# Forgetting attention in three units per head pair, output product joined to the next scores

## The reference, cut to what matters

```python
c = jnp.cumsum(log_f, axis=1)                 # forget gates, summed over the tokens
logits = einsum('bqhd,bkhd->bhqk', q_b * dh ** -0.5, k) + c_b[..., None] - c_k
logits = jnp.where(key_pos <= q_pos, logits, -inf)
o_fox = einsum('bhqk,bkhd->bqhd', softmax(logits), v)
...
o_fox = rms_norm(o_fox, fox_norm)             # over the 64 values of each head
h = h + concatenate([o_gla, o_fox]) @ w_out
```

## Time and profile before

| | |
|---|---|
| time, median of 3 | 2253.59 us (2252.46 to 2253.8) |
| the profiled execution | 2252.86 us |
| its span | 2251.6 us |
| TensorE busy | 2230.4 us, 99% of the span |
| VectorE, ScalarE busy | 63%, 47% |
| TensorE clock granted | 1.00 |

### The profile page before, as it was taken

How to read it: one execution, slowest core, us unless ns; L and a number is a source line. 1 busy time by engine, 2 the same in 40 slices (tenths; PEclk the granted TensorE clock), 3 DMA queues, 4 the chain that set the end, 5 groups by cost and what they waited for, 6 DMA issues and landing times.

```text
span 2251.6 us, 39369 instructions
## 1 busy us (share of the span) xinstructions
PE 2230.4 (99%) x15807; PEld 2025.2 (90%) x15807; DVE 1410.6 (63%) x2601; ACT 1048.9 (47%) x1963; POOL 118.3 (5%) x203
## 2 busy tenths in 40 slices
PE   9999999999999999999999999999999999999998
PEld 7798999999997898999899888978899888998997
DVE  5356576759743465667689566869455455863664
ACT  5356554447633465544377443223244444552652
POOL 3001010000000001100000010110000000000001
PEclk9999999999999999999999999999999999999999
DMA  6555676246434435732355262777721222543651
GB/s 222 163 130 148 179 190 184 98 141 174 137 94 127 121 112 142 185 118 96 112 174 167 87 181 82 192 188 216 197 66 64 67 95 86 154 156 117 182 165 51
DMA packets 97112, 313.01 MB, mean 139 GB/s; under 512 B 13809, under 2 KB 17811, under 8 KB 95907
## 3 DMA queue, kind: packets, MB, share of 16 engines
q1 hardware_dynamic: 84627, 220.93, 30.4%
q0 software_dynamic: 11584, 88.25, 16.9%
q10 hardware_dynamic: 720, 1.31, 0.2%
HBM read 308.32 MB, written 86.02 MB: 175 GB/s over the span
## 4 chain that ended last, share of the span: by engine, by line
PE 93%; DVE 3%; ACT 2%; issue 1%; DMA 0%; POOL 0%; SPq 0%; ACTq 0%; DVEq 0%; POOLq 0%
PE G L1427 58%; PE G L1464 15%; PE G L1543 7%; PE X L1464 3%; PE X L1755 1%; PE X L1710 1%; PE X L1840 1%; PE X L1733 1%; DVE wL L2432 1%; PE X L1824 1%; ACT wH L1893 1%; PE X L1503 1%; PE X L1809 1%; PE X L1427 1%; PE X L1796 0%
## 5 line engine op out<-in xcount | busy, mean ns | idle before, releaser
L1893 ACT ACTIVATE wH<-raw 128x512 fp32r<-128x512 f32 (+3 forms) x693 | 475.0, 704 | 468.8 <-PE G L1427 388.5
L2432 DVE TENSOR_TENSOR wL<-raw,wH 128x512 fp32r<-128x512 f32 (+3 forms) x693 | 538.3, 788 | 238.5 <-ACT wH L1893 235.1
L1427 PE MATMUL G<-aH,wH 128*128 128x264 f32 (+2 forms) x2000 | 503.0, 316 | 2.5 <-DVE aL L2445 2.0
L1427 PE MATMUL G<-aL,wH 128*128 128x264 f32 (+2 forms) x2000 | 481.7, 306 | 0.0
L1427 PE MATMUL G<-aH,wL 128*128 128x264 f32 (+2 forms) x2000 | 481.6, 306 | 0.0
L1427 PEld LDWEIGHTS G<-aH,wH 128*128 128x128 f32 x2000 | 324.5, 189 | 28.1 <-issue 6.0
L1427 PEld LDWEIGHTS G<-aH,wL 128*128 128x128 f32 x2000 | 322.4, 188 | 17.2
L1427 PEld LDWEIGHTS G<-aL,wH 128*128 128x128 f32 x2000 | 322.9, 188 | 14.4 <-issue 0.2
L1464 PE MATMUL G<-seven,wH 128*128 128x256 f32 (+2 forms) x960 | 177.5, 284 | 1.6 <-DVE wL L2432 1.5
L2591 DVE TENSOR_TENSOR hT<-G,hT 128x528 f32<-128x528 f32 (+1 forms) x83 | 58.0, 699 | 183.0 <-PE G L1427 183.0
L1464 PEld LDWEIGHTS G<-seven,wH 128*128 128x128 f32 x960 | 148.1, 188 | 3.7 <-issue 2.9
(11 more groups left out here) (407 smaller groups left out, 3911.0 us busy)
## 6 DMA issues: line engine op xcount, KB each, us to landing
raw<-weights SPq DMA_DIRECT2D x195, 512.0 KB, 3.8
weight_sums<-weights POOLq DMA_DIRECT2D x72, 704.0 KB, 6.4
raw<-weight_sums SPq DMA_DIRECT2D x160, 256.0 KB, 2.9
raw<-weights SPq DMA_DIRECT2D x48, 704.0 KB, 4.1
raw<-weights SPq DMA_DIRECT2D x121, 256.0 KB, 2.9
weight_sums<-weight_sums POOLq DMA_DIRECT2D x24, 704.0 KB, 5.2
weight_sums<-weights POOLq DMA_DIRECT2D x24, 448.0 KB, 4.9
raw<-weights SPq DMA_DIRECT2D x12, 384.0 KB, 5.4
```

The source lines that it names most:

```text
L1427: done = e.matmul(m.pair(i)[0:M, bank, 0:n], a[:, k, 0:M], b[:, kx, lo - t0:lo - t0 + n], start=(k == 0 and c == 0), stop=(k == nk - 1 and ...
L1893: e.activation(m.high(i)[:, c], m.raw(i)[:, c], ACT.Copy).then_inc(s.w_hi, 1)
L2432: e.tensor_tensor(m.low(i)[:, c], m.raw(i)[:, c], m.high(i)[:, c].bitcast(F32), ALU.subtract).then_inc(s.w_lo, 1)
```

## The change

- `FOX` groups the tiles into three units a pair, u = 0 to 11: kind 0 is tiles 1 and 2 in one (tile 2's scores at column 160 of the same bank), kind 1 is tile 3, kind 2 tile 4. Kind 0's scores, exponentials and normalisations have three pieces a head (144, 272 and the 16 meta queries).
- The transposes of both heads are taken in rounds of four: 3, 2 and 3 rounds for 12, 8 and 10 tiles (`fox_tiles`, `fox_rounds`). `PT` has 12 places for one unit, and the first round's copy waits for the output product of the unit before.
- The slots are laid anew: the output product of u - 1 and the scores of u stand in one slot, then the two normalisations, then the rounds. The norm of a pair is laid into unit 0 of the next pair: `nsq` in slot 2, the sums in slots 3 and 4, `ftail` with the last round.
- `fmeta` follows the scores of kind 1. Steps that waited in `late` are placed by `last_query()`.
- The rate is RATE_PAIR 0.75 until pair 0 is done and RATE_FOX 0.67 after it.

The diff, cut to its core. The lines that it takes out of `fs`, `ft` and `fo` stand in the kernel above; waits elsewhere only change their counts, for 12 units in a layer instead of 16:

```diff
-RATE_STATE, RATE_OUT, RATE_FOX, RATE_INDEX, RATE_HEADS = 0.5, 0.75, 0.8, 0.33, 0.62
+RATE_STATE, RATE_OUT, RATE_PAIR, RATE_FOX, RATE_INDEX, RATE_HEADS = 0.5, 0.75, 0.75, 0.67, 0.33, 0.62
...
+FOX = ((1, 0), (2, 160)), ((3, 0),), ((4, 0),)
+def fox_tiles(u):
+    out = []
+    for hh in range(2):
+        for i, at in FOX[u % 3]:
+            out += [(hh, i, -1, 144)] * (i == 1) + [(hh, i, j, at + TOK[j][0]) for j in range(i + 1)]
+    return out
+def fox_row(u):
+    return 2 * (u % 3 == 1)
+def fox_rounds(u):
+    return -(-len(fox_tiles(u)) // 4)
...
+        def last_query():
+            if ("mix", 4) in done and ("out of", ("fq", l, 3)) in done:
+                for what in late:
+                    step(*what)
+                late.clear()
...
-            for w in range(18):
-                p, i = w // 4, w % 4 + 1
-                if w < 16:
+            for u in range(13):
+                p, kind = u // 3, u % 3
+                if u < 12:
                     while ("fq", l, p) not in done:
                         yield "blocked"
-                    step("fs", l, w)
-                    if i == 1 and 1 <= p < 3:
+                if u:
+                    step("fo", l, u - 1)
+                if u < 12:
+                    step("fs", l, u)
+                    if kind == 0 and 1 <= p < 3:
                         step("sums", l, 2 * p + 2)
                         step("sums", l, 2 * p + 3)
-                    if i == 4:
+                    if kind == 1:
+                        step("fmeta", l, u)
+                    if kind == 2:
                         done.add(("pair", p))
                 yield
-                if 1 <= w < 17:
-                    step("ft", l, w - 1, 0)
+                if kind == 0 and p:
+                    step("nsq", l, p - 1)
+                if u < 12:
+                    step("fn", l, u, 0)
+                last_query()
                 yield
-                if i == 3 and p:
+                if kind == 0 and p:
+                    step("nsum", l, p - 1, 0)
+                if u < 12:
+                    step("fn", l, u, 1)
+                last_query()
+                yield
+                if kind == 0 and p:
                     step("nsum", l, p - 1, 1)
+                for r in range(fox_rounds(u) if u < 12 else 0):
+                    step("ft", l, u, r)
+                    if kind == 0 and r == 2 and p:
+                        step("ftail", l, p - 1)
+                        done.add(("mix", 3 + p))
+                    last_query()
                     yield
-                if 2 <= w:
-                    step("fo", l, w - 2)
-                if w < 16:
-                    step("fn", l, w, 0)
-                yield
-                if 1 <= w < 17:
-                    step("ft", l, w - 1, 1)
-                if i == 3 and w < 16:
-                    step("fmeta", l, w)
-                    if w == 10:
-                        assert ("out of", ("fq", l, 3)) in done
-                        for what in late:
-                            step(*what)
-                        late.clear()
-                if i == 3 and p:
-                    step("ftail", l, p - 1)
-                    done.add(("mix", 3 + p))
-                if w < 16:
-                    step("fn", l, w, 1)
-                yield
-                if i == 1 and p:
-                    step("ft", l, w - 1, 2)
-                    yield
-                if i == 2 and p:
-                    step("nsq", l, p - 1)
-                    yield
-                    step("nsum", l, p - 1, 0)
-                    yield
-            step("nsum", l, 3, 1)
-            yield
             step("ftail", l, 3)
             done.add(("mix", 7))
         done.difference_update([x for x in done if x in ("state", "out") or x[0] in ("pair", "mix")])
-        run(fg(), bg(), lambda: RATE_FOX if "out" in done else RATE_OUT if "state" in done else RATE_STATE)
+        run(fg(), bg(), lambda: (RATE_FOX if ("pair", 0) in done else RATE_PAIR) if "out" in done else RATE_OUT if "state" in done else RATE_STATE)
...
+                self.PT = sb("PT", [128, 12, 128], F32, cf)
...
+        pieces, diagonal = [], []
+        for i, at in FOX[kind]:
+            t0 = TOK[i][0]
+            pieces.append((t0, 0, t0 + 128, at) if i < 4 else (t0, NM, 512, 0))
+            diagonal.append((at + t0 if i < 4 else t0 - NM, 128))
+        if kind == 0:
             pieces.append((0, 0, NM, 144))
-        if i == 3:
+            diagonal.append((144, NM))
...
+        tiles, t = fox_tiles(u)[4 * r:4 * r + 4], fox_round(l, u, r)
+        e.wait_ge(s.f_norm, 2 * (12 * l + u) + tiles[-1][0] + 1)
+        if (u, r) == (0, 0):
             e.wait_ge(s.gn_ln, 4 * l + 4)
         else:
             e.wait_ge(s.f_pt, t)
-        if r < 2:
-            tiles = [(r, 144)] * (i == 1) + [(r, TOK[j][0]) for j in range(min(i + 1, 4))]
-        else:
-            tiles = [(hh, TOK[4][0]) for hh in range(2)]
-        for q, (hh, at) in enumerate(tiles):
-            done = e.transpose(X[:, 2, 128 * q:128 * q + 128], m.Sb[:, 2 * (n % 2) + hh, at:at + 128], m.ident[:, :])
+        for q, (hh, _, _, at) in enumerate(tiles):
+            done = e.transpose(X[:, 2, 128 * q:128 * q + 128], m.Sb[:, fox_row(u) + hh, at:at + 128], m.ident[:, :])
...
+        tiles = fox_tiles(u)
+        one = len(tiles) // 2
+        for q in range(one):
+            _, i, j, _ = tiles[q]
+            at = 0 if j < 0 or kind else TOK[i][0]
+            nq = NM if j < 0 else 128
             for hh in range(2):
                 c = 128 * p + 64 * hh
-                done = e.matmul(X[64 * hh:64 * hh + 64, 3, at:at + nq], m.fv[:, j, c:c + 64],
-                                m.PT[:, 2 * (n % 2) + hh, t, 0:nq], start=first, stop=last)
-                if q == len(tiles) - 1:
+                done = e.matmul(X[64 * hh:64 * hh + 64, 3, at:at + nq], m.fv[:, max(j, 0), c:c + 64],
+                                m.PT[:, one * hh + q, 0:nq], start=(j <= 0), stop=(j < 0 or j == i))
...
+        nt = len(fox_tiles(u)[4 * r:4 * r + 4])
         e.wait_ge(s.ft, t + 1)
-        if w >= 2:
-            e.wait_ge(s.fo, 2 * n - 2)
-        if r < 2:
-            nt = 3 if i == 1 else min(i + 1, 4)
-            e.activation(flat(m.PT[:, b + r, 0:nt, :]), X[:, 2, 0:128 * nt], ACT.Copy).then_inc(s.f_pt, 1)
-        else:
-            e.activation(m.PT[:, b:b + 2, 4, :], halves(X[:, 2, 0:256]), ACT.Copy).then_inc(s.f_pt, 1)
-    def fs(l, w):
-        i, n = w % 4 + 1, 16 * l + w
+        if n and r == 0:
+            e.wait_ge(s.fo, 2 * n)
+        e.activation(flat(m.PT[:, 4 * r:4 * r + nt, :]), X[:, 2, 0:128 * nt], ACT.Copy).then_inc(s.f_pt, 1)
...
+                e.activation(row[:, 160:432], row[:, 160:432], ACT.Exp, bias=sc[:, 7:8], scale=-1.0,
+                             accum_out=sc[:, 8:9]).then_inc(*own.one())
+            main = row[:, 0:TOK[FOX[kind][0][0]][0] + 128]
...
+            e.tensor_scalar(row[:, 160:432], row[:, 160:432], sc[:, 9:10], None, ALU.mult).then_inc(*own.one())
```

More of the change, by code:

```diff
@@ L295, with fox_round @@
 ENTRIES, WEIGHT_AT, MADE, READY, SUMS_SIZE = weight_places()
+FOX = ((1, 0), (2, 160)), ((3, 0),), ((4, 0),)
[9 more added lines that the diff above has]
+    return -(-len(fox_tiles(u)) // 4)
+def fox_round(l, u, r):
+    return sum(fox_rounds(v) for v in range(u)) + r + l * sum(fox_rounds(v) for v in range(12))
 def schedule():
@@ L599, in fg @@
                     yield from fm()
-            while ("mix", 5) not in done:
+            while ("mix", 5) not in done or late:
                 yield
-            assert not late
             yield from fm(before={1: ("mixin", l, 5)})
@@ L1683, in gn, with fs @@
         e.matmul(X[:, 3, 0:n], m.ones[:, :], m.gt[:, 1, 0:n], start=True, stop=True).then_inc(s.gn, 1)
[L1688 to L1691 removed]
+    def fs(l, u):
+        p, kind, n = u // 3, u % 3, 12 * l + u
+        if kind == 0:
             e.wait_ge(s.k_lo, 4 * l + p + 1)
             e.wait_ge(s.q_lo, 4 * l + p + 1)
[L1694 removed]
+        if u == 0:
             e.wait_ge(s.mix_gla, 8 * l + 8)
@@ L1745, in fo @@
             e.wait_ge(s.f_out, n)
-        if i == 1 and p:
+        if kind == 0 and p:
             e.wait_ge(s.n_ln, 2 * (4 * l + p))
[L1748 to L1752, removed]
+        e.wait_ge(s.f_pt, fox_round(l, u, fox_rounds(u) - 1) + 1)
+        tiles = fox_tiles(u)
[4 more added lines that the diff above has]
+            nq = NM if j < 0 else 128
             for hh in range(2):
                 c = 128 * p + 64 * hh
-                done = e.matmul(X[64 * hh:64 * hh + 64, 3, at:at + nq], m.fv[:, j, c:c + 64],
-                                m.PT[:, 2 * (n % 2) + hh, t, 0:nq], start=first, stop=last)
-                if q == len(tiles) - 1:
+                done = e.matmul(X[64 * hh:64 * hh + 64, 3, at:at + nq], m.fv[:, max(j, 0), c:c + 64],
+                                m.PT[:, one * hh + q, 0:nq], start=(j <= 0), stop=(j < 0 or j == i))
```

(50 more changed lines are left out.)

53 lines of the change are left out of this document (21 added, 32 removed).

## The result

The changed kernel takes 2285.19 us (median of 4 runs, 2284.51 to 2285.87), the kernel before 2253.4 us beside it: a ratio of 1.0141, 95% interval 1.0129 to 1.0153. It is slower, as forecast, but by 32 us where 12 were forecast, and the range ended at 2278.

A forecast was written before the change was run, and what follows sets the result against it. The prediction took TensorE, busy 2230.4 of 2251.6 us, as the bound. Losses of 24.6 us less a gain of 12.5 (work saved 9.7, old waits 2.8) gave net +12.1: 2265.7 us, range 2249 to 2278.

The forecast's parts named there:

- (a): Norm's first sum, pairs 0 to 2 of each layer: TensorE waits for the square behind ScalarE's exponentials, 14.4 us lost.
- (b): Norm's second sum beside the first transposes: their copy waits behind logarithm and exponential on ScalarE, 4.2 us lost (1.5 to 6).
- (d): Scores to transposes in the other 18 units: weight splits make eight normalisations late, 4 us lost (0 to 18).
- (c): Between transpose rounds: with one k-step between, the next waits 0.13 us for the copy, 2 us lost (0 to 5).
- Work saved: TensorE's attention steps: fewer score and output-product groups, joins, fewer transpose rounds, second sum beside transposes; 9.7 us saved.
- the join: Output product directly before the next scores, 22 times: 0.10 us each, one mode change remaining, 2.2 us saved (0 to 8).
- The norm's second sum beside the transposes: The norm's second sum right beside a round of transposes, six times: 0.5 us saved.
- Rival 3: Much slower, latency everywhere: (d) at its upper part, 16 us instead of 4, giving 2278 us; chance 0.14.
- The list of signs: Profile after: nsum waits about 2 us each, merged scores about 1.4, adjacent pair, TensorE's time without waits down 9 to 10.

The follow-up runs named there:

- fill: The changed kernel with short bf16 products put on TensorE ahead of its eight longest waits in each layer, nothing else changed: 2277.53 us, ratio to before 1.0106.
- halves: The changed kernel's merging and joins, but two units in flight, rates 0.60 and 0.56, and ScalarE's second-head exponentials one slot later: 2246.08 us, ratio to before 0.9966.
- rate: The changed kernel with attention slots closer, rates 0.85 and 0.80 instead of 0.75 and 0.67: 2286.97 us, ratio to before 1.0145.
- nsq: The changed kernel with the norm's square one slot earlier, ahead of the exponentials on ScalarE: 2272.4 us, ratio to before 1.0083.
- nsqhalves: The kernel nsq with ScalarE's exponentials parted, the second head's one slot later, one unit in flight: 2262.98 us, ratio to before 1.0040.

## Why the prediction was wrong

Right in sign and in its first mechanism; wrong in size, by one term that it did not have and two that it had too small. It put the waits at 24.6 us, and 27.8 were measured; most of the missing 20 us is TensorE running slower, which it had at nothing: the clock (9) and small delays (7). Two of its sums are off by 0.2 (six splits of 0.63 are 3.8, not 3.6; six waits of 1.0 or 0.3 in equal parts are 3.9, not 3.7), which changes nothing.

- **(a) The norm's first sum**: forecast 14.4 us for six, measured 14.0, with the predicted count, place and queue. The exponentials too took what was forecast (2.40 us for 2.48). That the sum fits so closely is partly luck. The forecast had a split behind the exponentials each time, 2.4 a wait. In layer 0 the wait was 2.10 with one split there, 3.28 with a mixin, a rest and a split, and 1.59 with nothing.
- **(b) The norm's second half**: forecast 4.2. The copy behind logarithm and exponential cost 0.66 at four of six places, where the second round started 1.99 after the first (215.77 to 217.76) and one k-step lay between. At the other two, two k-steps lay between and nothing was waited for. About 3 in all. Right within its bounds.
- **(d) Scores to transposes elsewhere**: forecast 4, measured 9.8. The step that failed was "taken nearer the low end as TensorE's other waits let the queues catch up". Half of it, 2.5 us twice, is the first unit of each layer, with four k-steps between its scores and its transposes. Behind the six exponentials ScalarE had two weight splits, and on VectorE the low half of the first split, which waited for the high one, stood ahead of the normalisation. No wait of TensorE over 0.2 us stands ahead of this one in the stage, so the queues had had no time to catch up (the lines below). The other eight waits, none over 0.8, sum to 4.8, near the forecast.

```profile
137.73 0.40 ACT L2321 ACTIVATE Sb<-Sb,sm 128x144 f32<-128x144 f32 x1
...
138.13 1.13 ACT L1908 ACTIVATE wH<-raw 128x512 fp32r<-128x512 f32 x2
...
138.77 0.69 DVE L2445 TENSOR_TENSOR wL<-raw,wH 128x512 fp32r<-128x512 f32 x1 [2.40 <-ACT wH L1908]
...
140.09 0.28 DVE L2976 TENSOR_SCALAR Sb<-Sb,sm 128x144 f32<-128x144 f32 x1
...
140.42 1.11 PE L1746 MATMUL X<-ident,Sb 128*128 128x128 f32 x4 [2.50 <-DVE Sb L2976]
```

- **(c) Round to round**: forecast 2. Of the 22 single k-steps between two rounds in the trace after, 16 take 1.02 or 1.03 and four 0.97 instead of 0.82, without a wait in the records: 3.8 us. Single k-steps between a round and an output product, 0.97 to 1.03 for 0.91, and similar cases add to it. By the sum below about 7 us of such small delays lie in busy time.
- **The clock, missing.** The prediction held the clock for constant, since the earlier trace rows show 1.00. At the three longest waits of each layer (2.50, 2.10 and 3.28 in layer 0) the granted clock falls to 0.50, its lower level of 1.2 of 2.4 GHz, for about 3 us each. The steps there take 1.4, 1.6 and 1.5 us longer than the same steps elsewhere: 4.5 a layer, 9 us. In the first, 0.3 of it may be a wait for the second head's row, as the same k-step is longer in `fill` too. Filling the idle stretches while leaving their cause took 9.3 us off TensorE's other work and gave back 7.7 (`fill`).
- **Work saved**: forecast 9.7, and `halves`, with no falls of the clock, shows 9.3 less busy time. By the steps of the trace the join was worth 0.20 and not 0.10 (22 x 0.20 = 4.4). The drain that the Trainium skill ("TensorEngine Tiling (Array Packing)", Key Properties) names costs nothing to be seen between an output product and scores: the bodies take 1.36 and 1.08 joined as well as with k-steps between. So its reading in the prediction, that a join keeps one change, does not hold here. The norm's second sum beside the transposes saved nothing (0.45 instead of 0.25).

The sum for the span's 33.0: waits 27.8 - 2.8 = 25.0, clock 9.0, small delays some 7, work -9.3, together 32. The small delays are what is left over in this sum, but `fill` supports their size: without its products its busy time is 2228.1, and `halves`, with nearly the same work and a clock of 1.00 as well, has 2221.1.

Rival 3, "latency everywhere" at 0.14, had the right direction for (d), not the clock. The list of signs held: nsum's waits at u = 3, 6 and 9, the merged scores of 1.43, the adjacent pair. The one that failed was "TensorE's time without the waits down by 9 to 10": it rose by 7.0.

Open: why closer slots made so few waits longer in `rate`, what decides whether the clock falls behind a given idle stretch, and the price of a join apart from distances.

## What to carry to other kernels

Where a stage is hidden behind a saturated engine, price a reordering by what stands ahead of each waited-for instruction in the queue of the engine that serves it, not by the distance on the saturated engine alone. Merging units saves edges but makes the block in the helper's queue longer: part it by head, and let the previous unit's short copy go in between. And reckon with slow steps behind an idle stretch of some 2 us on TensorE. All six of 2.10 to 3.28 us in the changed kernel cost about half as much again, but not every such stretch did in the other runs.

## Not expected of the hardware

The granted clock fell within one stage, for about 3 us at a time (0.57 in the window 140 to 144 us, 0.61 in 212 to 216), with idle stretches of 2.10, 2.50 and 3.28 us and not with those of 0.80 or 1.59. On the whole run the falls show only as 0.995. 128-column bf16 products of 0.0575 us each, back to back, were enough to keep it at 1.00.

The length of the idle stretch alone does not decide it. In `nsq` a wait of 2.50 is followed by a fall in layer 0 and the same wait in layer 1 is not; in `rate` one of 2.75 is followed by none. In `nsq` a fall came 1.7 us after a wait of only 1.73, and `nsqhalves` has a wait of 1.73 and no fall. The first two windows are from `nsq`, behind the wait of 2.50 in layer 0 and in layer 1, the third from `rate`, behind the one of 2.75:

```profile
140.50:143.30 2.80, 2.75 (x13) 2.76 (x14) 1.48 (x7) 0.60 (x1) 0.00 (x0) 0.50 0.43 132
...
796.50:800.00 3.50, 3.36 (x27) 3.15 (x28) 1.43 (x7) 1.20 (x2) 0.00 (x0) 1.00 0.47 150
...
866.48:869.00 2.52, 2.52 (x17) 2.29 (x18) 2.45 (x14) 1.44 (x3) 0.40 (x1) 1.00 0.91 286
```
